# Half of the samples' depthwise convolution on GpSimd, between its gathers

## What is computed

```python
def conv_mix(x, buf, w_pw1, b_pw1, w_dw, b_dw, ln_g, ln_b, w_pw2, b_pw2):
    """Conformer conv module, causal. x: (B,T,D); buf: (B, CONV_WIDTH-1, D) past GLU rows."""
    D = x.shape[-1]
    h = x @ w_pw1 + b_pw1
    u = h[..., :D] * jax.nn.sigmoid(h[..., D:])
    full = jnp.concatenate([buf.astype(u.dtype), u], axis=1)
    c = lax.conv_general_dilated(full, w_dw[:, None, :].astype(full.dtype), window_strides=(1,),
                                 padding='VALID', dimension_numbers=('NWC', 'WIO', 'NWC'),
                                 feature_group_count=D) + b_dw
    ...
    out = jax.nn.silu(cn) @ w_pw2 + b_pw2
    return out, full[:, -(CONV_WIDTH - 1):]

def peer(x, w_q, sub_keys, u_tab, v_tab):
    ...
        act = jax.nn.gelu(jnp.einsum('bhkd,bd->bhk', u_tab[idx], xb).astype(jnp.float32), approximate=False)
        return jnp.einsum('bhk,bhkd->bd', (gate * act).astype(xb.dtype), v_tab[idx])
```

## Time and profile before

| | us |
|---|---|
| median of 3 runs | 3850.49 (3847.30 to 3853.64) |
| profiled execution, device time | 3850.32 |
| its span in the trace | 3848.5 |

### The profile page before, as it was taken

How to read it: one execution, slowest core, us unless ns; L and a number is a source line. 1 busy time by engine, 2 the same in 40 slices (tenths; PEclk the granted TensorE clock), 3 DMA queues, 4 the chain that set the end, 5 groups by cost and what they waited for, 6 DMA issues and landing times.

```text
span 3848.5 us, 56215 instructions
## 1 busy us (share of the span) xinstructions
PE 2857.6 (74%) x20248; PEld 1343.3 (35%) x20248; DVE 2727.9 (71%) x6400; ACT 1449.0 (38%) x4376; POOL 1423.6 (37%) x1272
## 2 busy tenths in 40 slices
PE   7899998697666667788869657798786666666655
PEld 4667766442222212343324213344232222222211
DVE  5666665467666667777787767888776777777774
ACT  1333332134333334454444334444443333333333
POOL 0111111144444444444444444343344444444442
PEclk9999998897888878898889779999898877878777
DMA  2111110499999999999999999999999999999996
GB/s 79 36 31 27 43 31 18 159 426 426 427 426 426 427 427 426 418 388 402 408 426 422 426 425 426 389 383 373 397 416 426 426 425 427 427 426 426 425 426 283
DMA packets 230360, 1313.42 MB, mean 341 GB/s; under 512 B 58816, under 2 KB 62016, under 8 KB 82368
## 3 DMA queue, kind: packets, MB, share of 16 engines
q0 software_dynamic: 165888, 1208.03, 75.0%
q1 hardware_dynamic: 64192, 101.79, 7.5%
HBM read 1303.88 MB, written 5.86 MB: 340 GB/s over the span
## 4 chain that ended last, share of the span: by engine, by line
DMA 37%; PE 19%; DVE 18%; ACT 3%; issue 3%; DVEq 1%; ACTq 1%; POOL 1%; POOLq 0%
DMA arena<-in_uv,arena 37%; DVE arena L1780 9%; PE psum L1352 8%; PE psum L1314 4%; PE psum L1404 3%; PE psum L1434 2%; DVE arena L1869 1%; ACT wbuf L1570 1%; ACT arena L1565 1%; PE psum L1424 1%; DVE arena L1708 1%; POOL arena L1294 1%; DVE arena L1843 1%; DVE arena L1705 1%; DVE level L1732 0%
## 5 line engine op out<-in xcount | busy, mean ns | idle before, releaser
L1352 PE MATMUL psum<-arena,wbuf 64*64 64x512 f32 (+1 forms) x8704 | 1456.4, 743 | 864.5 <-ACT wbuf L1570 844.0
L1294 POOL DMA_INDIRECT arena<-in_uv,arena x1152 | 1344.2, 1167 | 1773.7 <-PE psum L1352 1571.7
L1780 DVE SCALAR_TENSOR_TENSOR arena<-arena 128x1024 f32<-128x1024 f32 x1152 | 1395.9, 1223 | 577.1 <-DMA arena<-in_uv,arena 550.4
L1352 PEld LDWEIGHTS psum<-arena,wbuf 64*64 64x64 f32 (+1 forms) x8704 | 336.1, 155 | 1759.9 <-ACT wbuf L1570 1364.1
L1561 ACT ACTIVATE arena<-arena 128x2 f32<-128x2 f32 x576 | 117.0, 203 | 1664.7 <-DVE arena L1780 1644.6
L1570 ACT ACTIVATE wbuf<-cst,arena 128x64 f32<-128x64 f32 x1152 | 338.1, 340 | 41.6 <-issue 2.4
L1314 PE MATMUL psum<-arena,wbuf 128*128 128x256 f32 (+1 forms) x1024 | 308.4, 449 | 8.4 <-DVE arena L1791 5.8
L1565 ACT ACTIVATE arena<-arena 128x1 f32<-128x1 f32 x1152 | 276.7, 287 | 41.5 <-issue 2.1
L1314 PEld LDWEIGHTS psum<-arena,wbuf 128*128 128x128 f32 x1024 | 201.6, 207 | 172.4 <-issue 130.7
L419 PE MATMUL psum<-arena,wbuf 128*128 128x288 f32 x672 | 189.0, 415 | 2.8 <-ACT arena L705 2.8
L1036 POOL COPY x<-arena 128x256 f32<-128x256 f32 x8 | 3.2, 397 | 423.2 <-DVE x L883 423.2
(11 more groups left out here) (273 smaller groups left out, 3155.4 us busy)
## 6 DMA issues: line engine op xcount, KB each, us to landing
wbuf<-in_w_q SPq DMA_DIRECT2D x64, 576.0 KB
arena<-in_w_pw SPq DMA_DIRECT2D x48, 512.0 KB
arena<-in_uv,arena POOLq DMA_INDIRECT x1152
wbuf<-in_w_rkv SPq DMA_DIRECT2D x24, 512.0 KB, 4.2
wbuf<-in_w_o SPq DMA_DIRECT2D x8, 512.0 KB, 3.7
arena<-in_w_o SPq DMA_DIRECT2D x8, 512.0 KB
x<-in_x SPq DMA_DIRECT2D x5, 576.0 KB, 6.1
arena<-in_state SPq DMA_DIRECT2D x16, 128.0 KB, 2.9
```

Source lines behind the costliest of these rows:

```text
L1294: pool.indirect_dma_start(ring[:, g % RING, :], None, I["uv"][p // 2], bass.IndirectOffsetOnAxis(ap=idx[:, s % 4, j:j + 1], axis=0)).then_ ...
L1352: last = pe.matmul(ps[e * HD:(e + 1) * HD, 2 * (u % 2) + a if u < NB else 4, :], diag[t, g % DIAGS, :], ring[t, g % RING, D + e * 512:D + ...
L1780: stt(out=row, in0=row, scalar=1.0, in1=tok[p % 2][:, UNITS[p % 2].index(u), :], op0=ALU.mult, op1=ALU.mult, accum_out=dots[:, g % COLS:g ...
```

## The change

Four of the eight sample positions of every chunk leave VectorE and are computed on GpSimd, between its gathers, as four multiplications, then a tree of additions (31 products to 15 + 1, then 8, 4, 2, 1) and the bias. GpSimd waits for `glu` of the chunk and, between dependent steps, for its own semaphore `conv_sample_step`; its steps are placed in rows that are counted behind the ring (row g - 11 when it gathers row g). A new semaphore, `conv_sampled`, is waited for by SyncE (before it loads new past rows), VectorE (before the `glu` of the chunk after next) and TensorE (before `add_up`). VectorE keeps the other four positions, now at row at+2, in a buffer of their own. In half B TensorE takes 13 of the prompt's taps instead of 16 and ScalarE makes 13 diagonals; VectorE takes 18 taps instead of 15 in the same seven rows. Half A's split stays at 16 and 15.

```diff
@@ GpSimd: the new function and where it is stepped @@
+            def samples(n, t):
+                summed = 0
+                for c in range(C):
+                    at = t["conv"] + c * t["chunk"] + 1
+                    us = uss[c % 2]
+                    weight = unsq(K.par[:, TAP0:TAP0 + TAPS, c], 1, SB)
+                    bias = K.par[:, B_DW, c:c + 1].unsqueeze(1).to_broadcast([P, HT, SB])
+                    yield from tick.until(at)
+                    pool.wait_ge(dve_b.sem, dve_b.value(f"{n}.glu{c}"))
+                    for e in (0,):
+                        out = cv[1][:, c, 2 * P:WIDTH[1]].rearrange("p (b t) -> p t b", t=ST)
+                        for i in range(HT):
+                            last = pool.tensor_tensor(prods[:, i], us[:, :, e * HT + i:e * HT + i + TAPS], weight, ALU.mult)
+                            if i < HT - 1:
+                                yield from tick.until(at + 4 * e + (i + 1) // 3)
...
+                        for i in range(0, HT, 2):
+                            last = pool.tensor_tensor(prods[:, i:i + 2, :, 0:15], prods[:, i:i + 2, :, 0:15], prods[:, i:i + 2, :, 16:31], ALU.add)
+                        for m in (8, 4, 2, 1):
...
+                            yield from tick.until(at + 4 * e + (2 if m == 8 else 3))
+                            pool.wait_ge(sample_step, summed)
+                            last = pool.tensor_tensor(prods[:, :, :, 0:m], prods[:, :, :, 0:m], prods[:, :, :, m:2 * m], ALU.add)
...
+                        last = pool.tensor_tensor(out[:, e * HT:(e + 1) * HT], prods[:, :, :, 0], bias, ALU.add)
+                    last.then_inc(sampled, 1)
...
+                    if p == 2:
+                        tick.now = g - RING - PHASE_ROW[2]
+                        next(work, None)
@@ SyncE, TensorE and VectorE: the new waits @@
+                            sp.wait_ge(sampled, c - 1)
...
-                    for k in range(PE_TAPS):
+                    for k in range(PE_TAPS[half]):
...
+                    if half:
+                        pe.wait_ge(sampled, c + 1)
...
+                        if c >= 2:
+                            dve.wait_ge(sampled, c - 1)
@@ VectorE: the samples @@
-                        for e in range(2):
-                            yield from tick.until(at + 1 + 2 * e)
-                            sample_taps(c, us, e)
-                        rest = cv[half][:, c, 2 * P:w]
-                        ts(rest, rest, K.par[:, B_DW, c:c + 1], None, ALU.add)
+                        yield from tick.until(at + 2)
+                        sample_taps(c, us)
```

More of the change, by code:

```diff
@@ L1073, in retrieval_and_conv @@
     RING, DIAGS, LEAD, COLS = 11, 8, 2, 12
-    PE_TAPS = 16
+    PE_TAPS = (16, 13)
     HALFK = TOPK // 2
@@ L1165, in retrieval_and_conv @@
     pe_b, act_b, dve_b = Steps(K.sem("bg_pe"), pe_names), Steps(K.sem("bg_act"), act_names), Steps(K.sem("bg_dve"), dve_names)
+    sampled, sample_step = K.sem("conv_sampled"), K.sem("conv_sample_step")
     last_out = ("n0A", "n0B", "n1A", "n1B")
@@ L1296, in _ @@
                                             ).then_inc(here[g % RING], 16)
+                    if p == 2:
+                        tick.now = g - RING - PHASE_ROW[2]
+                        next(work, None)
+                if s + 1 == len(SEQ) or SEQ[s + 1][0] == 3:
+                    tick.now = 10 ** 6
+                    for _ in work:
+                        pass
         @block.tensor
@@ L1433, in taps @@
                             q = slice(e * HD, e * HD + HD)
-                            last = pe.matmul(part[q], tap_diags[q, k, :], ups[c % 2][q, k:k + 2 * P], start=k == 0, stop=k == PE_TAPS - 1)
+                            last = pe.matmul(part[q], tap_diags[q, k, :], ups[c % 2][q, k:k + 2 * P], start=k == 0, stop=k == PE_TAPS[half] - 1)
                     last.then_inc(pe_b.at(f"{n}.tapped{c}"), 1)
@@ L1836, in glu, with sample_taps @@
                         dve.drain()
[L1838 removed]
+                def sample_taps(c, us):
                     weight = unsq(K.par[:, TAP0:TAP0 + TAPS, c], 1, SB)
                     for i in range(ST // 2):
[L1842 to L1843 removed]
+                        at = ST // 2 + i
+                        tt(prods_d[:, i], us[:, :, at:at + TAPS], weight, ALU.mult)
                     dve.drain()
[L1845 to L1846 removed]
+                    out = cv[half][:, c, 2 * P:w].rearrange("p (b t) -> p t b", t=ST)[:, ST // 2:ST, :]
+                    dve.tensor_reduce(out=out, in_=prods_d, op=ALU.add, axis=AX.X)
                     dve.drain()
+                    ts(out, out, K.par[:, B_DW, c:c + 1], None, ALU.add)
                 if half == 0:
@@ L1866, in conv @@
                     spread = t["chunk"] - 6
-                    for k in range(PE_TAPS, TAPS):
-                        yield from tick.until(at + 5 + (k - PE_TAPS) * spread // (TAPS - PE_TAPS))
+                    for k in range(PE_TAPS[half], TAPS):
+                        yield from tick.until(at + 5 + (k - PE_TAPS[half]) * spread // (TAPS - PE_TAPS[half]))
                         last = stt(out=out, in0=up[:, k:k + 2 * P], scalar=K.par[:, TAP0 + k, c:c + 1], in1=out, op0=ALU.mult, op1=ALU.add)
```

14 lines of the change are left out of this document (13 added, 1 removed).

## The result

The changed kernel takes 3858.24 us (median of 20 runs, 3853.31 to 3864.13) where the kernel before takes 3851.32 us on the same chip (20 runs, 3845.61 to 3854.52 but for one of 3868.45 and one of 4244.96). The ratio is 1.0018, with a 95% interval of 1.0011 to 1.0026: 0.18% slower, 6.9 us. The forecast was 3861 us.

The account below looks back on a forecast made before the run. VectorE was taken to bound the kernel only in half B's 325 us convolution. VectorE's work -14.5, exclusion +22 and tap-sum wait +3 gave +10.5 us on 3850.3: 3861 us, range 3840 to 3874.

Parts of the forecast that it names:

- The bound: In half B's convolution, 325 us, VectorE is the bound at 89% busy; transfers nearly full, leaving 10 to 15 us at most.
- The sum: Over half B's convolution: -14.5 us of VectorE work, +22 of exclusion and +3 of tap-sum wait make +10.5 us.
- VectorE's own work: Half B's chunks: a samples' group of 3.50 us leaves, three prompt taps of 1.69 us come; -14.5 us for eight chunks.
- GpSimd's instructions: Eleven new GpSimd instructions a chunk, between gathers, take 5.5 to 6.1 us; the four multiplications 2.5 to 3.1 of it.
- Delay of the gathers: GpSimd's gathers may run some 5 us late on four rows of 13; costed at nothing, landed rows being cover.
- The exclusion: GpSimd instructions reading SBUF and VectorE's two-SBUF-input ones block each other: 2.8 us a chunk, 22 us for eight, bounds 0 to 49.
- The tap sum: VectorE reaches row at+5 earlier than TensorE's tap sum is ready, and waits 0.4 us more a chunk, 3 us in all.
- Rival 1: In half B's convolution the engines miss each other and VectorE is relieved until transfers bind: 3836 to 3841 us, chance 0.20.
- The signs that I had named: In half B's convolution: longer dot products and taps beside GpSimd's multiplications, their minimum near 0.62 us, stretch about 335 us, tap-sum wait 12 to 18.
- wrong central term: Exclusion in half B's convolution; disproved by dot products staying at 1224 ns, a stretch under 315 us, or one waiting for a gather.
- what the prediction called measurable: For the whole kernel's time, a difference under 0.2% (7.7 us) is about what can be told from none: 3842.8 to 3858.2 us.

Follow-up runs that it names:

- no_pool: The changed kernel with GpSimd's eleven instructions a chunk replaced by one small memset, half of the samples' sums left out; 3844.0 us, ratio to the kernel before 0.9984.
- late_wait_b: The kernel before, with TensorE's wait for half B's projection weights placed in the row where they are used instead of two rows ahead; 3846.6 us, ratio 0.9992.
- mults_twice: The changed kernel with GpSimd doing its four multiplications a chunk twice, in one burst before the first additions; 3871.0 us, ratio to the kernel before 1.0056.
- the late wait: TensorE's wait for half B's projection weights moved to the row of use; alone on the kernel before 3846.6 us, with dense samples' weights 3842.8 us.
- spread: The changed kernel with GpSimd's eleven instructions a chunk placed one behind each gather instead of in bursts; 3869.5 us, ratio to the kernel before 1.0053.

## Why the prediction was right

Each step as the prediction put it:

- **The bound.** VectorE in the convolution of half B, and nothing else: right. Outside that stretch the traces agree. The sum said +10.5 us; the stretch grew by 9.9 us, the profiled execution by 7.8 and the median by 6.9.
- **VectorE's own work, -14.5 us:** right. Without GpSimd's arithmetic it is busy 15.3 us less.
- **GpSimd's instructions, 5.5 to 6.1 us a chunk:** low. With each at the shortest of its kind in the changed kernel, the eleven take 7.0 us. The multiplication with the weights' step takes 0.83 us at its shortest, so four of them are 3.3 us, not 2.5 to 3.1, and the additions are longer too (240 columns take 0.70 us at the least, not 0.61). The prediction's estimate of 3.6 us for the four, which by its own 177 ns and 1.79 ns a column should read 3.4, was the nearer one, but not for the step alone: with dense weights they take 682 ns each, where the sum had 621. The step of eight costs GpSimd 850 - 682 = 168 ns an instruction and VectorE 194 ns, which is more than I read out of the earlier trace rows, where I had compared two different operations.
- **Delay of the gathers, nothing:** right, and shown: in the changed kernel one dot product waits for a gather, before GpSimd's first multiplication, and no_pool has the same wait of 1.3 us.
- **The exclusion, 22 us:** right in kind, low in size. VectorE is busy 308.0 - 280.7 = 27.3 us more than without it, 3.4 us a chunk. I had taken 80% of 3.5 us. The share was about right, and the lengths were not: by the same rule (a GpSimd instruction costs its own length less 0.19 us) the measured lengths give 7.0 - 11 x 0.19 = 4.9 us a chunk if each meets a victim, and 3.4 is 70% of it. Of the 27.3 us the prompt taps have 16.4 and the dot products 4.5. I also left out small victims in the expert search, which have 3.5 us together: an instruction of 16 columns with two inputs (L1791, 1.19 us in the second chunk instead of 0.18) and the `TENSOR_SCALAR` of 16 columns (L1778), with one input, which took 2.20 us beside a burst of three multiplications instead of 0.17 (its line in the changed kernel, in the convolution, stands below). The Trainium skill (SBUF — State Buffer, § Who interferes with whom) names `tensor_scalar` among the operations that can contend with GpSimd for the shared pair of ports when their operands meet certain conditions. By that rule, the trace agrees in this one instruction of six, the only one that started beside GpSimd's arithmetic.

```profile
L1778 DVE TENSOR_SCALAR arena<-arena x6: 174/174/2200, 2440.0 to 2697.2; 128x16 uint32<-128x16 uint32 x6
```

- **The tap sum, +3 us:** too high, and with the gate's wait the sign turns. The tap sum's wait rose by 1.4 us and the gate's fell by 4.2; with the 1.3 us for a gather VectorE waits 1.5 us less than before. That fits a VectorE that is slowed and so comes later to both (in no_pool, where it is not slowed, they are 17.1 and 8.1 us), but this is argued and not shown. The two errors (+5 us on the exclusion, -4.5 on the waits) cancel: that the forecast lies only 2.8 us from the measured time is in part luck.
- **Rival 1** (3836 to 3841 us if the engines miss each other) was too fast: no_pool is that case and takes 3844. The transfers did not stop it, as I had it (their share is 0.97 in its stretch, below the 0.98 of before); the waits did. VectorE got 15.3 us back and waited 10.2 us more. Its longest wait, 7.5 us for a gate at 2515 us, comes behind TensorE's standstill of 15.1 us that ends at 2497 us. In no_pool the trace does not name what TensorE stood for; in late_wait_b it is the weights, at the same place. That the standstill makes VectorE wait is argued from this order and not shown.

The signs that I had named: dot products of up to 1.7 us and taps of up to 0.9 us. They reach 2.17 and 1.62 us, since one instruction can wait for more than one of GpSimd's. The tap-sum wait (12.8 us) and the lengthening of the stretch (9.9 us for about 10) came as named; GpSimd's multiplications have a minimum of 0.83 us and not 0.62. One sign of a wrong central term did come, a dot product that waits for a gather, 1.3 us. It does not speak against the exclusion, since no_pool has it too; as a sign it was drawn too wide. The size of the difference, 0.18%, lies at the edge of what the prediction called measurable; with 20 runs of each kernel the interval excludes no difference.

## What to carry to other kernels

Arithmetic on GpSimd is not free beside a VectorE that works on two SBUF inputs. Here GpSimd's two-input instructions, 56 us at their shortest, cost VectorE 27 us in bursts and 35 spread out; copies cost 3 us and writes nothing. Ask first how much of what leaves the bounding engine comes back as its waits; here a relief of 15 us shortened the stretch by 6 and a load of 11 us lengthened it by 6, while further on (mults_twice over the changed kernel) 11.5 us cost 10.6, each read from one trace. And look at the operand's step before looking for another engine: dense weights took a third off the same instructions on VectorE (a fifth on GpSimd), and together with the late wait they beat both kernels.

## What the runs showed of the hardware

- A VectorE instruction can wait for a whole burst of GpSimd instructions, not only for the one in progress: 2.96 us for an instruction of 0.69 us beside three multiplications of together 2.44 us.
- GpSimd instructions that only write (memsets) add nothing to VectorE's two-input instructions (1222 and 484 ns with 672 of them between). Its one-input copies add 3.1 us in all, and wait themselves: 577 ns on the mean instead of 397 for 256 columns.
- VectorE's one-input searches (`MAX8`, `FIND_INDEX8`) overlapped GpSimd's arithmetic 20 times in spread and were never more than 8 ns longer for it. A one-input `TENSOR_SCALAR` was, once, from 174 to 2200 ns. The samples' reduction (1188 ns) never met it in any run, so its constant length shows nothing.
- A second operand read with a step of eight floats takes VectorE from 410 to 604 ns and GpSimd from 682 to 850 ns for 248 columns.
